# Who makes the gate-scaled identities of a product-key retrieval block: GpSimd, two groups ahead, in place of VectorE

## What is computed

```
def peer_ffn(x, w_query, sub_keys, expert_u, expert_v):      # x: 1024 tokens, blocks of 128
    q = (tb @ w_query).reshape(128, 8 heads, 2, 64)
    s = einsum('thpd,hpnd->thpn', q, sub_keys)               # 128 keys per half
    s1, i1 = top_k(s[:, :, 0], 16);  s2, i2 = top_k(s[:, :, 1], 16)
    top_s, pos = top_k(all 256 sums of s1 and s2, 16)        # 16 experts per head
    idx = the experts of pos                                 # out of 16384
    g = softmax(top_s)
    u = expert_u[idx]
    act = gelu(einsum('thkd,td->thk', u, tb))
    coef = g * act
    return einsum('thk,thkd->td', coef, expert_v[idx])
```

## Time and profile before

| what | value |
|---|---|
| three runs | 3007.16 us median, 3000.02 to 3017.94 |
| the profiled execution, its own time | 3005.16 us |
| its span, first to last instruction | 3003.3 us |
| TensorE clock granted, mean | 0.859 |
| busy: PE, DVE, POOL, ACT | 75%, 73%, 44%, 38% |
| moved by DMA | 1161.02 MB, of it 1073.81 MB by POOL's gathers |
| mean DMA rate over the span | 387 GB/s |

### The profile page before, as it was taken

The page is one execution under the profiler, slowest core; times in us unless marked ns, Lnnn a source line. Parts: engine busy times, 40 slices in busy tenths (PEclk is TensorE's granted clock), DMA queues, the critical chain, the costliest instruction groups (busy, mean ns, idle before and its releaser), DMA issues.

```text
span 3003.3 us, 30584 instructions
## 1 busy us (share of the span) xinstructions
PE 2243.7 (75%) x8860; PEld 938.3 (31%) x8860; DVE 2186.0 (73%) x5486; ACT 1142.5 (38%) x2665; POOL 1316.5 (44%) x1126
## 2 busy tenths in 40 slices
PE   7987878788887888877788688877755676555556
PEld 6564332244432454322322133212311132111111
DVE  4157887677776777759888887869876887768655
ACT  3422356633454334543277235853212331121111
POOL 0013444534455344544456444654444454444442
PEclk9998988889988999888889788978877888777777
DMA  7359999999999999999999999999999999999997
GB/s 289 114 184 374 396 368 383 376 385 385 404 401 402 393 393 398 395 388 419 417 416 414 418 413 415 394 417 419 417 415 419 419 393 419 419 420 409 417 420 325
DMA packets 203431, 1161.02 MB, mean 387 GB/s; under 512 B 24032, under 2 KB 57696, under 8 KB 71808
## 3 DMA queue, kind: packets, MB, share of 16 engines
q0 software_dynamic: 147456, 1073.81, 87.6%
q1 hardware_dynamic: 55808, 85.26, 7.8%
HBM read 1142.13 MB, written 16.84 MB: 386 GB/s over the span
## 4 chain that ended last, share of the span: by engine, by line
DMA 33%; PE 29%; DVE 20%; ACT 8%; issue 6%; POOL 2%; SPq 1%; POOLq 0%; ACTq 0%; DVEq 0%
DMA r_uv<-in_experts,r_wk 30%; PE ps L1764 13%; DVE r_uv L1375 9%; PE ps L1480 4%; PE ps L1671 2%; PE ps L1690 2%; ACT r_uv L1007 2%; POOL r_uv L755 2%; PE ps L1474 2%; DMA oa_dram<-r_wk 2%; ACT L1004 1%; PE ps L1496 1%; DVE r_wk L1285 1%; DVE r_wk L1283 1%; DVE r_wk L1286 1%
## 5 line engine op out<-in xcount | busy, mean ns | idle before, releaser
L755 POOL DMA_INDIRECT r_uv<-in_experts,r_wk x1024 | 1213.0, 1185 | 1482.8 <-PE ps L1764 1207.6
L1764 PE MATMUL ps<-r_uv 128*64 128x512 f32 x4096 | 1268.7, 753 | 707.7 <-ACT r_uv L1007 684.7
L1375 DVE CUSTOM_DVE_ANT_0 r_uv<-r_uv,hnrep 128x1024 f32<-128x1024 f32 x1024 | 1250.1, 1236 | 565.3 <-DMA r_uv<-in_experts,r_wk 556.8
L1764 PEld LDWEIGHTS ps<-r_uv 128*64 128x64 f32 x4096 | 296.1, 160 | 1482.0 <-ACT r_uv L1007 985.1
L1004 ACT ACTIVATE r_wk<-r_wk 128x2 f32<-128x2 f32 x512 | 104.0, 203 | 1513.2 <-DVE r_wk L1375 1512.0
L1007 ACT ACTIVATE r_uv<-gid,r_wk 128x64 f32<-128x64 f32 x684 | 200.6, 340 | 11.5
L1004 ACT ACT_TABLE_LOAD x137 | 175.8, 1283 | 2.5
L777 ACT ACT_TABLE_LOAD x117 | 150.1, 1283 | 23.1 <-PE ps L1653 13.7
L1480 PE MATMUL ps<-r_uv,stream_chunk 128*128 128x256 f32 x576 | 142.0, 402 | 9.8 <-DMA stream_chunk<-in_w_chunks 9.6
L1690 PEld LDWEIGHTS ps<-r_wk,r_wq 128*128 128x128 f32 x1024 | 119.6, 193 | 40.6 <-issue 40.2
L1480 PEld LDWEIGHTS ps<-r_uv,stream_chunk 128*128 128x128 f32 x576 | 112.4, 200 | 59.0 <-issue 43.6
(11 more groups left out here) (167 smaller groups left out, 2104.2 us busy)
## 6 DMA issues: line engine op xcount, KB each, us to landing
r_uv<-in_experts,r_wk POOLq DMA_INDIRECT x1024, 13.0
stream_chunk<-in_w_chunks SPq DMA_DIRECT2D x31, 512.0 KB, 8.0
r_wk<-lkv_dram SPq DMA_DIRECT2D x72, 128.0 KB, 7.3
r_uv<-in_x SPq DMA_DIRECT2D x8, 512.0 KB, 10.5
r_wo<-in_w_chunks SPq DMA_DIRECT2D x8, 512.0 KB, 11.3
r_wk<-in_x SPq DMA_DIRECT2D x8, 512.0 KB, 8.0
r_wo<-in_w_out SPq DMA_DIRECT2D x8, 512.0 KB, 9.5
r_wq<-in_w_query SPq DMA_DIRECT2D x8, 512.0 KB, 7.3
```

The costliest lines, as they stand in the source:

```text
L755: g.indirect_dma_start(uv[:, SLOT[G], :], None, experts, bass.IndirectOffsetOnAxis(idx[b % 2][:, k:k + 1], 0)).then_inc(rows_in[SLOT[G]], 16)
L1375: v.tensor_tensor_reduce(uv[:, slot, 0:D], uv[:, slot, 0:D], hnrep[:, k % GRP, :], 1.0, 0.0, ALU.mult, ALU.add, actv[:, k:k + 1]).then_inc ...
L1764: last = t_.matmul(ps[HALF * j:HALF * j + HALF, i, :], uv[:, slot, 0:HALF], uv[:, slot, D + 512 * i:D + 512 * i + 512], start=n == 0, stop ...
```

## The change

`gated_ident` moves from DVE's program to POOL's, word for word but for the engine. POOL runs it for group n - 2 behind the two gathers of group n (and for group 0 and 1 behind those of group 3). The last two identities come behind the last gather. The waits move with it: `routed` where a part of the gates begins, and `diag_ready` for the buffer. The number of buffers, the ring, the dot products, ACT's and PE's programs stay as they are.

```
+AHEAD = 3
...
@@ in the program of POOL
+            def gated_ident(m):
+
+                b, n = m // NG, m % NG
+                for i, (h0, h1) in enumerate(PARTS[b]):
+                    if n == TOPK // GRP * h0:
+                        gate(pool, "pool", routed, part_number(b, i))
+                if m >= 3:
+                    gate(pool, "pool", diag_ready, GRP * (m - 2))
+                g.tensor_tensor(gid[m % 3][:, :, :], ident64.unsqueeze(1).to_broadcast([P, GRP, HALF]),
+                                gates[b % 2][:, GRP * n:GRP * n + GRP].unsqueeze(2).to_broadcast([P, GRP, HALF]),
+                                ALU.mult).then_inc(gid_ready, 1)
...
                     g.indirect_dma_start(uv[:, SLOT[G], :], None, experts,
                                          bass.IndirectOffsetOnAxis(idx[b % 2][:, k:k + 1], 0)
                                          ).then_inc(rows_in[SLOT[G]], 16)
+                    n = NG * b + k // GRP
+                    if k % GRP == GRP - 1 and n >= AHEAD:
+                        if n == AHEAD:
+                            gated_ident(0)
+                        gated_ident(n - AHEAD + 1)
                     if late is not None and k % GRP == GRP - 1:
...
             for b in range(NT):
                 gathers_of(b, LATE_OF[b] if b < len(LATE_OF) else None)
+            for m in range(NG * NT - AHEAD + 1, NG * NT):
+                gated_ident(m)
@@ in the program of DVE
-            def gated_ident(m):
...
                 if b:
                     dve.wait_ge(dotted, K * b)
                     repeat_rows()
-                else:
-                    gated_ident(0)
...
                                                    ALU.mult, ALU.add, actv[:, k:k + 1]).then_inc(dotted, 1)
-                        if NG * b + n + 1 < NG * NT:
-                            gated_ident(NG * b + n + 1)
```

## The result

The changed kernel takes 3094.95 us (median of 4 runs, 3087.13 to 3099.17), the kernel before 3009.85 us beside it (4 runs, 3000.02 to 3017.94). The ratio is 1.0281, with a 95% interval of 1.0243 to 1.0320: slower by 2.8%, 85 us. 3074 was forecast, with a range of 3004 to 3120. The profiled execution took 3087.13 us, 8 us under that median, and 82 us more than the profiled one of before (3005.16).

The account below looks back on a forecast made before the run. No engine is full; DMA engines bound the wide ring and nearly the narrow one, where POOL's gathers hang on PE. Chain +75, relief -8: +67 on 3005.2 makes 3072, plus 2 to the median 3074 us; range 3004 to 3120.

Parts of the forecast that it names:

- the ring did not absorb it: Rival, narrow ring: gathers already queued swallow PE's lateness of a few us; 3005 us, no change; chance 0.13.
- relief: Rival, block 0 and narrow-stretch bursts: DVE without identities no longer falls behind; 2987 us, faster; chance 0.07.
- contention rival: Narrow ring: identities wait for DVE instructions, 0.4 us more, chain 6.2 us, time 3130 us; chance 0.13.
- The length of the chain, 5.8 us: Seven slots, once per group: three matmuls 1.75, release 1.25, gather 1.18, sequencer 0.30, identity 0.54, ACT's diagonals 0.59, hand-overs 0.12 and 0.05.
- narrow stretch: Groups 56 to 191 on seven slots, 795 us before; forecast about 75 us longer.
- the 1.25 for the release: Narrow ring: from the end of PE's third matmul to the start of POOL's gather, taken as 1.25 us.
- the forecast's shortest form: Seven slots: chain of 5.0 us, with matmuls at full clock, an unheld gather (0.93) and an identity of 0.33.
- The cost of the chain, +75 us: Narrow ring, 136 groups: no PE spacing under 5.8 us; +62 to +105 us, +75 taken.
- the two ways of counting: Narrow ring: short spacings raised and longer ones kept, 0.77 us per group; two long ones' waits shrinking, 0.46.
- The twelve spacings: Narrow ring: PE's group spacings in the earlier trace, 2.71 to 8.82 us, mean 5.66; raising six short ones costs 9.3 us.
- DVE's relief, -8 us: DVE loses its identities: 6 us gained in block 0 (groups 0 to 55), 2 us in late bursts afterwards; between 0 and 20.
- What was expected to be free: Zero cost: wide ring (groups 192 to 511, DMA share 1.01), identity 0 at the start, the `routed` wait, held dot products.

## Why the prediction was right

**Which ring, and which group.** The forecast put the loss on the seven-slot ring through one wait, that of the gather ahead of the identity. Moving the identity by one gather removes it, moving only those 136 identities brings all of it, and one more group of lead on nine slots makes it anew. Of the rivals none is left as the main cause: the ring did not absorb it, relief is worth some 9 us, and the kernel with the identity between the gathers has the same instructions without the loss. The forecast's own contention rival was a chain made 0.4 us longer by collisions. A part of that is there: an identity takes 0.42 us in the middle case and 0.62 on average, but not the 0.94 (0.54 and 0.4) of that rival.

**The length of the chain, 5.8 us.** By the changed kernel's own rows in the narrow stretch:

```profile
L1768 PE MATMUL ps<-r_uv 128*64 128x512 f32 x1104 | 341.9, 751 | 198.7 <-ACT r_uv L1027 198.4
```

```profile
L768 POOL DMA_INDIRECT r_uv<-in_experts,r_wk x276 | 326.2, 1182 | 415.2 <-PE ps L1768 387.6 <-issue 26.3 <-ACT r_uv L1027 0.3
L748 POOL TENSOR_TENSOR gid<-cst,r_wk 128x128 f32<-128x128 f32 x92 | 58.3, 634 | 1.7
...
L748 POOL TENSOR_TENSOR cst<-cst,r_wk 128x128 f32<-128x128 f32 x46 | 26.9, 584 | 0.8
```

Three quarters of 341.9 / 136 are 1.89 us (forecast 1.75). The gather is 1.18 (1.18), the identity 0.62 (0.54), and behind the gather it starts at once (0.02, as in the turn shown, where I had put 0.30). With the forecast's 1.25, the 0.59 and the small hand-overs of 0.10 and 0.05, that is 5.7. The straight line through the 512 and 256 wide additions was a fair guide to the mean of a 128 wide operation.

These are means over all groups. In the 69 that the chain holds, the steps are 2.14 us for the three matmuls, 1.46 from the third to the gather, 1.11, 0.02, 0.62, 0.10, 0.59 and 0.06, together 6.1. So the forecast was 0.3 low there: the matmuls were slower, and the 1.25 for the release, which had no row of its own (the gather of the earlier trace rows stood behind another gather), is about the least seen (1.23), not the mean. The missing gap of 0.30 made up for half of these two. The chain is also not one number but lies between 4.84 and 7.75 us; its least is near the 5.0 of the forecast's shortest form. The sentence that no spacing can be under 5.8 does not hold: 42 of 136 are, down to 3.90.

**The cost of the chain, +75 us in the sum, measured +85.** The narrow stretch grew by 85 between its first dot products. That lies between the two ways of counting (+62 and +105). The twelve spacings were a fair sample: raising all 136 of the kernel before to 5.8 gives +105 as well. What the waits in front of long groups give back was a guess, 30 of the 105; 20 came back, and which waits gave them is not shown. So the place and the mechanism were worked out, and that +75 came within 10 us owes something to luck.

One thing was not in the sum: the granted clock of TensorE in the stretch fell from 0.90 to 0.86, and the same 1104 matmul records took 341.9 us instead of 318.3. That is 0.17 us per group, 0.13 of it inside the chain. How much of the 85 us it makes is not shown: with POOL inside the narrow ring alone the clock was 0.88 and the stretch as long.

The whole forecast was +67 on the profiled execution, and +82 came: 10 of the 15 between them are the narrow stretch and 5 the front part. Most of the rest of the way from 3074 to 3095 is that the profiled execution of the change was 8 us under its median.

**DVE's relief, -8 us, spread over block 0 and the rest.** The kernel without identities gives -9 by its ratio. In the change, block 0 shows -4, with a DMA share of 0.97 instead of 0.95, and the rest from group 192 on -4. These agree with the sum, but do not show it: block 0 takes 326 to 333 us in the kernels that make its identities on POOL, against 330 before, and 332 and 328 in two executions of one kernel. The split into 6 and 2 us stays open.

**What was expected to be free.** On the wide ring the identities cost nothing, as forecast: POOL is busy 1061 of 1638 us there instead of 797. The first eight gathers hid identity 0; POOL stood 2.2 us for `routed` in front of it, where I had put nothing, and it was still made 7 us before the first dot product.

**One forecast of the profile failed.** I expected a DMA share near 0.91 on the narrow ring, by dividing the same busy time by a longer stretch. It was 0.95, while the rate did fall by the full tenth, from 394 to 356 GB/s. The step that failed took the share for a measure of bytes. The same step is in the 20 us that bound the relief in block 0: by the rates of the earlier trace rows, 375 against 415 GB/s, it would be 32.

## What to carry to other kernels

When an operation is moved into an in-order engine that also issues the loads, look at what the load in front of it waits for: the operation for group n should not stand behind a load whose slot group n - 1 frees. Here the load ahead of it was that of row 2n + 5. With 8 slots that load waits for row 2n - 3, the last of group n - 2; with 7 it waits for row 2n - 2, the first of group n - 1. Where a ring changes its size, check at the smallest, and move the operation forward in the order, by as little as one instruction.

## What the runs showed of the hardware

- **Under the chain, the clock was lower too.** Four matmuls of a group take 1.94 us at 2.4 GHz and 3.68 at 1.2 GHz; in the earlier trace rows a slow one at 845.76 (granted clock 0.50, the lower level, from 845.8 to 849.2) follows an idle time of 4.44 us, while the one at 827.27 (0.50 too) has none right in front of it. On the wide ring the granted clock was 0.83 in the changed kernel and 0.73 in the one with the long lead there, whose PE was busy 1262 of 2034 us (62%) instead of 1118 of 1638 (68%). Its matmul records took 880 ns on average, against 776 ns in the changed kernel. That the idle time brings the lower clock, and so lengthens the chain once more, is likely from this and was not tried apart:

```profile
L1768 PE MATMUL ps<-r_uv 128*64 128x512 f32 x2537 | 812.5, 776 | 510.6 <-ACT r_uv L1027 494.3 <-DVE h2cur L1354 15.9
```

- **A gather is held by a dot product, and POOL's identities make that longer on the wide ring.** Before the change, 344 gathers begin with over 0.15 us of a dot product left, and 316 of them end 0.79 to 0.83 us after it, as the one of the earlier trace rows does. On the wide ring the mean gather was 1191 ns over 633 before, and 1301 ns over 634 in the change, 70 us in all, without any cost in time:

```profile
L755 POOL DMA_INDIRECT r_uv<-in_experts,r_wk x633 | 753.9, 1191 | 837.3 <-PE ps L1764 706.2 <-issue 130.0
```

```profile
L768 POOL DMA_INDIRECT r_uv<-in_experts,r_wk x634 | 824.7, 1301 | 566.8 <-PE ps L1768 416.5 <-issue 80.0 <-ACT r_uv L1027 66.8
```

About as many gathers begin inside a dot product there (321 and 303 of 640), but those take 1.60 us on average instead of 1.38. On the narrow ring the mean stayed at 1.18. DVE's dot products on the wide ring went from 1229 to 1253 ns. The identity itself took 418 ns in the middle case and 625 ns on average in `gid`; on DVE the middle case was 287 ns. And DVE, which lost 512 identities in both, is busy 2114 us in the change (2101 to 2124 in the seven kernels that make them all on POOL) and 2070 us in the kernel without identities. That the 44 us go into being held by POOL is likely and was not tried apart.
- **The DMA share overstates how full the queues are.** 356 GB/s read as 0.95 and 394 as 0.99 on the same kind of work.
